# Delta-rule recurrence: level masks put on the products by VectorE, and another order of side work

## What is computed

```python
def rwkv7_branch(z, mu, w0, w_up, a0, a_up, k_k, k_a, r_k, ln_g, ln_b):
    z = token_shift_mix(z, mu)
    r, k, v, g, wd, ad = split_cols(z, RWKV_COLS)
    w = jnp.exp(-DECAY_SCALE * jax.nn.sigmoid((w0 + jnp.tanh(wd) @ w_up).astype(f32)))
    a = jax.nn.sigmoid((a0 + ad @ a_up).astype(f32))
    ...
    kk = kk / jnp.maximum(jnp.linalg.norm(kk, axis=-1, keepdims=True), 1e-12)
    k = k * (1.0 + (a - 1.0) * per_head(k_a))

    def step(state, inp):
        r_t, w_t, k_t, v_t, kk_t, a_t = inp
        sa = jnp.einsum('bhvk,bhk->bhv', state, -kk_t)
        state = (state * w_t[:, :, None, :]
                 + sa[..., None] * (kk_t * a_t)[:, :, None, :]
                 + v_t[..., None] * k_t[:, :, None, :])
        return state, jnp.einsum('bhvk,bhk->bhv', state, r_t)
    ...
    _, y = lax.scan(step, s0, (...))
```

## Time and profile before

| | us |
|---|---|
| median of 3 runs | 4497.86 |
| lowest, highest | 4497.32, 4507.33 |
| profiled execution | 4503.45 |
| its span, first to last instruction | 4502.2 |

### The profile page before, as it was taken

One profiled execution on the slowest core, in us unless ns is written; L12 is line 12 of the kernel. 1 busy time (PEld: TensorE's weight loads), 2 busy tenths in 40 slices (PEclk: granted clock), 3 DMA queues, 4 the chain that ended last, 5 costly groups with the idle time before them and its releaser, 6 DMA issues. The chain is left out here.

```text
span 4502.2 us, 55986 instructions
## 1 busy us (share of the span) xinstructions
PE 3841.9 (85%) x22256; PEld 2253.5 (50%) x22256; DVE 1901.7 (42%) x4026; ACT 1023.9 (23%) x2215; POOL 573.3 (13%) x412
## 2 busy tenths in 40 slices
PE   7699816699999998899986787699899986887698
PEld 1464413344444444565654776344565654776344
DVE  0223375411002111278874553332278974553332
ACT  0321103300001100230123444122230123444122
POOL 0000004200000000002301331110002301331110
PEclk9799958899999999899998888799999998888799
DMA  6212253322442243213321004320213321004320
GB/s 227 89 45 81 76 162 113 132 70 89 149 159 84 82 161 112 69 43 89 94 74 59 25 27 129 113 70 14 65 42 89 94 74 59 25 27 140 102 71 19
DMA packets 226967, 387.52 MB, mean 86 GB/s; under 512 B 33178, under 2 KB 135970, under 8 KB 225706
## 3 DMA queue, kind: packets, MB, share of 16 engines
q1 hardware_dynamic: 217558, 374.11, 25.1%
q10 hardware_dynamic: 9168, 9.98, 0.7%
HBM read 297.11 MB, written 73.31 MB: 82 GB/s over the span
## 5 line engine op out<-in xcount | busy, mean ns | idle before, releaser
L3105 PE MATMUL win_acc<-win_wt,hTl 128*128 128x384 f32 (+3 forms) x3072 | 909.1, 457 | 18.0 <-DMA win_wt<-in_w_in 18.0
L3105 PEld LDWEIGHTS win_acc<-win_wt,hTl 128*128 128x128 f32 x3072 | 561.7, 191 | 360.0 <-DMA win_wt<-in_w_in 18.8
L1480 PE MATMUL mlp_bk<-hTl,mlp_w 128*128 128x512 f32 x1024 | 444.1, 596 | 22.4 <-DMA mlp_scale<-in_norm_g 22.4
L1502 PE MATMUL mlp_bk<-mlp_w,mlp_aT 128*128 128x512 f32 x1024 | 440.3, 592 | 2.3 <-ACT mlp_aT L1385 1.6
L2195 DVE TENSOR_SCALAR_CACHE_REDUCE win_rl<-d_sc,win_mid 128x384 f32<-128x384 f32 (+5 forms) x384 | 363.2, 946 | 40.1 <-DVE win_mid L2203 28.2
L1480 PEld LDWEIGHTS mlp_bk<-hTl,mlp_w 128*128 128x128 f32 x1024 | 195.7, 192 | 268.0 <-issue 245.3
L1502 PEld LDWEIGHTS mlp_bk<-mlp_w,mlp_aT 128*128 128x128 f32 x1024 | 194.2, 190 | 246.3 <-issue 246.3
L1287 DVE TENSOR_SCALAR mlp_r<-mlp_bk,mlp_b 128x512 f32<-128x512 f32 x64 | 48.1, 751 | 494.9 <-PE mlp_bk L1480 484.8
L2950 PE MATMUL tail_wo<-tail_w_out,tail_yT 128*128 128x512 f32 x512 | 234.2, 612 | 20.7 <-DVE tail_yT L2806 20.7
L420 PE MATMUL zin_acc<-zin_wt,hTl 128*128 128x512 f32 (+2 forms) x640 | 228.4, 512 | 0.0
L2961 PE MATMUL tail_wg<-tail_w_gate,tail_xT 128*128 128x512 f32 x512 | 224.4, 592 | 2.5 <-DVE tail_xT L2806 2.5
(11 more groups left out here) (442 smaller groups left out, 5792.7 us busy)
## 6 DMA issues: line engine op xcount, KB each, us to landing
mlp_w<-in_w SPq DMA_DIRECT2D x48, 2048.0 KB, 8.0
win_wt<-in_w_in SPq DMA_DIRECT2D x18, 1536.0 KB, 8.9
ada_w<-in_w_ada SPq DMA_DIRECT2D x12, 2048.0 KB, 7.6
s_z<-win_ot SPq DMA_DIRECT2D x14, 1536.0 KB, 7.2
hTl<-s_z SPq DMA_DIRECT2D x16, 832.0 KB, 4.6
win_zp<-win_ot SPq DMA_DIRECT2D x8, 1344.0 KB
zin_wt<-in_w_in SPq DMA_DIRECT2D x4, 2048.0 KB, 8.2
tail_w_out<-in_w_out SPq DMA_DIRECT2D x4, 2048.0 KB, 13.6
```

The source lines that it names most:

```text
L1480: mm = pe.matmul(bk[:, 4 * half + f % 2, :], wv[:, k, f * P:(f + 1) * P], hT[:, k, half * HT * P:(half + 1) * HT * P], start=k == 0, stop= ...
L1502: mm = pe.matmul(bk[:, bank(n0 + t_) + q, :], aT[:, 4 * c + f, group(2 * pair + t_)], wv[:, f, q * COL:(q + 1) * COL], start=c == 0 and f ...
L3105: mm = pe.matmul(acc[:, u % RING, 0:w], hT[:, k, t * P:(t + 1) * P], wt[:, i % 2, k, 0:w], start=k == 0, stop=k == KC - 1)
```

## The change

GpSimd no longer cuts L to its levels: `lower`, LT and its semaphore go. `make_P` multiplies the whole matrix that `first_pairs` leaves in mT (now I - L, written in place), and `take_P` multiplies the product by the level's mask, whose constant now holds the diagonal too. `first_pairs` computes I - L and then masks it, so it has two instructions as before. `ends` also waits for `r6_ready`, the last piece of `keys`. On VectorE the side work is in another order: exponents, three keys, take_tr, three keys, scaled; `rates(n+1)` goes ahead of the masks. `take_S` and `take_y` move to ScalarE. ScalarE's side work starts at step 3: two exponentials, take_r2, two exponentials, take_S 0, nothing, nothing, take_S 1, take_y; `low` goes ahead of `turn_in`. On TensorE `turn_low(n+1)` goes ahead of the turns and `low(n+1)` ahead of values. At the start, exponents(0) go ahead of keys(0).

```diff
             def _(gp):
-                def lower(n):
-                    for g in range(NG):
-                        hs = slice(2 * g, 2 * g + 2)
-                        gp.wait_ge(masked, START + n * RWH + 2 * g + 2)
...
-                        gp.tensor_tensor(LT[:, q, :, :], mT[:, n % 2, :, 0, :], bc_mid(levels[:, q, :], RWH), ALU.mult).then_inc(LT_ready, 1)
...
                 def ends(m):
...
+                    gp.wait_ge(r6_ready, START + m + 1)
                     gp.wait_ge(f_ready, START + m + 1)
...
                 gp.wait_ge(const_in, START + N_CONST * DMA)
-                ends(0)
                 for n in range(NT):
-                    lower(n)
-                    if n + 1 < NT:
-                        ends(n + 1)
+                    ends(n)
...
                 def first_pairs(n, g):
-                    TT = Tb[:, n % 2, g, 1, :, :]
+                    L = mT[:, n % 2, 2 * g:2 * g + 2, 0, :]
                     dve.wait_ge(masked, START + n * RWH + 2 * g + 2)
-                    tt(TT, mT[:, n % 2, 2 * g:2 * g + 2, 0, :], bc_mid(first[:, :], 2), ALU.mult)
-                    dve.tensor_tensor(TT, TT, bc_mid(id64[:, :], 2), ALU.add).then_inc(TT_first, 1)
+                    s(dve.scalar_tensor_tensor(L, L, -1.0, bc_mid(id64[:, :], 2), ALU.mult, ALU.add))
+                    dve.tensor_tensor(Tb[:, n % 2, g, 1, :, :], L, bc_mid(first[:, :], 2), ALU.mult).then_inc(TT_first, 1)
...
                 def take_P(n, k):
-                    g = k % NG
+                    q, g = divmod(k, NG)
                     dve.wait_ge(p_made, START + n * K + k + 1)
-                    dve.scalar_tensor_tensor(PS[:, 2 * g:2 * g + 2, :], blocks(bk[:, k % 2, 0:2 * HD]), -1.0, bc_mid(id64[:, :], 2),
-                                             ALU.mult, ALU.add).then_inc(p_out, 1)
+                    dve.tensor_tensor(PS[:, 2 * g:2 * g + 2, :], blocks(bk[:, k % 2, 0:2 * HD]), bc_mid(levels[:, q, :], 2),
+                                      ALU.mult).then_inc(p_out, 1)
...
                 def side(n):
                     ahead, behind = n + 1 < NT, n >= 1
-                    yield from keys(n + 1) if ahead else range(6)
+                    early = keys(n + 1) if ahead else iter(range(6))
+                    yield from exponents(n + 1) if ahead else range(4)
+                    yield from islice(early, 3)
                     yield from take_tr(n - 1) if behind else range(1)
-                    yield from exponents(n + 1) if ahead else range(4)
-                    yield from take_S(n - 1, 0) if behind else range(1)
-                    yield
-                    yield from take_S(n - 1, 1) if behind else range(1)
+                    yield from early
                     if ahead:
                         yield from scaled(n + 1)
-                    if behind:
-                        yield from take_y(n - 1)
...
                 rates(0)
+                for _ in exponents(0):
+                    pass
                 dve.wait_ge(const_in, START + N_CONST * DMA)
                 for _ in keys(0):
                     pass
-                for _ in exponents(0):
-                    pass
...
                 for n in range(NT + 1):
+                    if n + 1 < NT:
+                        rates(n + 1)
                     if n < NT:
                         mask(n, 0)
                         mask(n, 1)
                         first_pairs(n, 0)
-                    if n + 1 < NT:
-                        rates(n + 1)
-                    if n < NT:
                         mask(n, 2)
...
+                def take_S(n, c):
+                    pr, po = half(c)
+                    act.wait_ge(zeroed, START + 1)
+                    act.wait_ge(S_made, START + 2 * n + c + 1)
+                    act.activation(St[po, :], bk[po, 6, 0:RW], ACT.Copy).then_inc(S_ready, 1)
+                    yield
+
+                def take_y(n):
+                    act.wait_ge(S_made, START + 2 * n + 2)
+                    if n >= 4:
+                        act.wait_ge(stored[n % 4], START + n // 4 * DMA)
+                    act.activation(yo[:, n % 4, 0:RW], bk[:, 7, 0:RW], ACT.Copy).then_inc(y_read, 1)
+                    yield
...
                 def side(n):
-                    yield from take_r2(n - 1) if n >= 1 else range(1)
-                    yield
-                    yield
-                    yield
-                    if n + 1 < NT:
-                        yield from exps(n + 1)
+                    ahead, behind = n + 1 < NT, n >= 1
+                    curves = exps(n + 1) if ahead else iter(range(4))
+                    yield from islice(curves, 2)
+                    yield from take_r2(n - 1) if behind else range(1)
+                    yield from curves
+                    if behind:
+                        yield from take_S(n - 1, 0)
+                        yield
+                        yield
+                        yield from take_S(n - 1, 1)
+                        yield from take_y(n - 1)
...
                             for k in range(K):
                                 take_T(n, k)
-                                if k >= 4:
+                                if k >= 3:
                                     next(rest, None)
...
                 def make_P(n, k):
-                    q, g = divmod(k, NG)
-                    pe.wait_ge(LT_ready, START + (NG + LV - 1) * n + (g + 1 if q == 0 else NG + q))
+                    g = k % NG
...
-                            mm = pe.matmul(bk[pr, k % 2, col(h)], LT[pr, q, 2 * g + h, :], T_of(n, 2 * g + h, pr), start=True, stop=True)
+                            mm = pe.matmul(bk[pr, k % 2, col(h)], mT[pr, n % 2, 2 * g + h, 0, :], T_of(n, 2 * g + h, pr), start=True, stop=True)
...
                     ahead, behind = n + 1 < NT, n >= 1
+                    if ahead:
+                        turn_low(n + 1)
                     if n < NT:
                         turns(n)
                     if ahead:
-                        turn_low(n + 1)
+                        low(n + 1)
                     if behind:
                         values(n - 1)
```

More of the change, by code:

```diff
@@ L4 @@
 import numpy as np
-from itertools import chain
+from itertools import chain, islice
 import concourse.bass as bass
@@ L1621, in rwkv @@
         Tb = ph.sb("Tb", [P, 2, NG, 2, 2, HD])
-        LT, PS = ph.sb("LT", [P, LV, RWH, HD]), ph.sb("PS", [P, RWH, HD])
+        PS = ph.sb("PS", [P, RWH, HD])
         wv, uw = ph.sb("wv", [P, 3, RWH, P]), ph.sb("uw", [P, RWH, P])
@@ L1630, in rwkv @@
         names = ("wd_turned wdT_ready lowrank pre sig cums cums_out ex_ready fn_ready f_ready x4_ready "
-                 "r6_ready ext_ready turned xT_ready scores masked TT_first T_turned LT_ready p_made p_out t_made t_out "
+                 "r6_ready ext_ready turned xT_ready scores masked TT_first T_turned p_made p_out t_made t_out "
                  "dv_made dv_ready uw_made uw_ready half_made last_made tr_ready r2_ready S_made S_ready y_read zeroed").split()
         (wd_turned, wdT_ready, lowrank, pre, sig, cums, cums_out, ex_ready, fn_ready, f_ready, x4_ready,
-         r6_ready, ext_ready, turned, xT_ready, scores, masked, TT_first, T_turned, LT_ready, p_made, p_out, t_made, t_out,
+         r6_ready, ext_ready, turned, xT_ready, scores, masked, TT_first, T_turned, p_made, p_out, t_made, t_out,
          dv_made, dv_ready, uw_made, uw_ready, half_made, last_made, tr_ready, r2_ready, S_made, S_ready, y_read, zeroed) = (ph.sem(n) for n in names)
@@ L1938, in _ @@
                             turn_in(n, q)
-                    if n + 1 < NT:
-                        low(n + 1)
                     if 1 <= n <= NT:
@@ L1964, in turn_low @@
                     pe.wait_ge(in_[m % 4], START + (m // 4 + 1) * 2 * DMA)
+                    if m >= 1:
+                        pe.wait_ge(cums_out, START + m)
                     if m >= 3:
@@ L2129, in _ @@
                         score(n, 1)
-                    if ahead:
-                        low(n + 1)
-                    if n < NT:
                         score(n, 2)
@@ L3318, in constants_2 @@
     pair = (s // 2 == t // 2)
-    c["rw_first"] = -halves(pair & (s < t)).astype(f)
-    c["rw_levels"] = np.stack([halves((s // (2 * b) == t // (2 * b)) & (s % (2 * b) < b) & (t % (2 * b) >= b)) for b in (2, 4, 8, 16, 32)], 1).astype(f)
+    c["rw_first"] = halves(pair & (s <= t)).astype(f)
+    c["rw_levels"] = np.stack([halves((s // (2 * b) == t // (2 * b)) & (s % (2 * b) >= b) & (t % (2 * b) < b) | (s == t)) for b in (2, 4, 8, 16, 32)], 1).astype(f)
     c["causal_ts"] = np.where(t <= s, 0, -BIG).astype(f)
```

2 lines of the change are left out of this document (removed).

## The result

The change makes the kernel faster: a median of 4391.26 us (4387.34 to 4394.88, four runs) against 4500.44 for the kernel before in the same comparison, a ratio of 0.9755 with a 95% interval of 0.9738 to 0.9772. The gain is 109 us; 4414 was forecast, with 4394 as the low end of the range. The direction and the main mechanism held; the size of the gain was forecast too small.

What follows compares the result with a forecast made beforehand. TensorE's order of work bounds the recurrences. Per layer 5.0 + 20.7 + 16.5 + 1.5 + 0.7 - 0.65 = 43.75 us, twice 87.5, off 4503.45: 4416, given as 4414; range 4394 to 4458 for 8 in 10.

Steps and rivals of the forecast that it cites:

- What bounds the kernel: In the recurrences of both layers, TensorE's order of work is the path, and its gaps are what can be won.
- Masks: Level multiplies leaving GpSimd, some 95 us of its work: 0 gain outside the head, bounds 4 us either way.
- Chain of blocks 1 to 6: The 15 steps of make_P to take_T in six blocks per layer: 3.45 us less each, 20.7 per layer.
- First chain: The first block's chain, which has no chunks: 15.9 us against 20.9, 5.0 less per layer.
- Head: Turns, scores, low-rank and sums products before a chain: 1.2 us less by order, 1.55 by clock; six give 16.5 per layer.
- Last head: The eighth block's head: 1.5 us less per layer, from the clock alone.
- Clock: TensorE's longest idle stretch, 1.2 us before make_T(9), leaves the clock up; if up in the head, 1.55 us less there.
- the rival at 4436: Clock falls as before in the heads, taking back 1.55 us seven times per layer, 21.7; chance 0.25.
- The copies: State and output copies on ScalarE: hidden by the wait for scaled; without that cover up to 0.5 us a block.
- ScalarE as the bound: Its queue in steps 3 to 12 delays take_T and the last exponential: slower, 4547 us; chance 0.06.
- the table load: ScalarE's load before exponentials takes 1.28 us; the skill's 1.38 drain per switch would add 20 us in all, making 4434.
- The shorter wait: Scaled 1 goes earlier than C+14.6 (C: block's first make_P), tail at TensorE's pace: 1.5 us more per block, 4393; chance 0.10.

Runs made afterwards that it cites:

- The filled kernel: The kernel before with 12, 2 and 2 idle identity matmuls put ahead of make_T(12), (13) and (14), nothing left out: 4468.35 us, ratio 0.9929.

## Why the forecast was 23 us too high

- **What bounds the kernel**: right. TensorE's order is the path, and its gaps were what went. What paces the tail of the chain was wrong: the prediction had the steps behind make_T(9) "go by VectorE", and the 6.0 us from there to the next turns came out nearly right (5.8), although TensorE waited for VectorE only 0.5 us of them. Its own carry and steps take nearly as long; that is luck.
- **Masks**: 0 outside the head, with bounds of 4 us either way. Measured 8 us, and 1.3 of a layer's share (1.9 in the new order) in the first block, which has no chunks to hide it under. TensorE's waits for LT, on which I rested the 0, showed nothing of what GpSimd does to VectorE's durations. That shows in VectorE's 59.5 us too: 26.5 are the copies, and 16.7 of the rest two multiplies of `keys` that had run beside the masks. Groups by line (count, busy us, mean ns, idle), first before, then after:

```profile
L1730 DVE SCALAR_TENSOR_TENSOR rwkv_t<-rwkv_la,rwkv_rows 128x384 f32<-128x384 f32 x16 | 18.8, 1177 | 2.0 <-issue 2.0
```

```profile
L1716 DVE SCALAR_TENSOR_TENSOR rwkv_t<-rwkv_la,rwkv_rows 128x384 f32<-128x384 f32 x16 | 8.8, 549 | 0.0
```

- **Chain of blocks 1 to 6**: right. 3.45 each was forecast, 20.7 per layer; measured 22.1 and 21.2. The stretch that I took as 24.97 was 24.83 in most blocks, and the new one is 21.38 for 21.5.
- **First chain**: 5.0 forecast, 4.1 measured (20.64 to 16.53). I had read 20.9.
- **Head: the term that was mis-sized.** 2.75 a block, 16.5 per layer; measured 21.7 and 24.2. It failed twice. First, the base: the earlier trace rows shows the block at 2572.00 with 11.9, and that is the shortest of the twelve heads; their mean is 12.45. That is 0.55 twelve times, 6.6 us. Second, the new head: 9.15 forecast (11.9 less 2.75), 8.63 measured, 0.52 twelve times, 6.2 us. Against the mean head, 1.07 is missing: 0.65 of it the clock, 0.2 the order, and 0.2 between the two, which I put down to the masks. In the block that I read, the clock was back by 2576.0, 4 us into the head. In another, whose turns start at 2645.93, it came back later, as these half microseconds of the kernel before show:

```profile
2645.93:2646.43 0.50, 0.50 (x3) 0.50 (x4) 0.00 (x0) 0.00 (x0) 0.39 (x1) 0.50 0.80 293
...
2650.00:2650.50 0.50, 0.50 (x17) 0.50 (x19) 0.00 (x0) 0.04 (x1) 0.00 (x0) 0.50 0.00 0
2650.50:2651.00 0.50, 0.50 (x15) 0.34 (x8) 0.00 (x0) 0.48 (x2) 0.00 (x0) 0.80 0.00 0
```

  There it is some 4.8 us into the head, and that head took 12.46; over the twelve heads it is 3.6 to 5.4 us. The filled kernel shows the whole price, 2.2, for the 1.55 that I took as half of three operations. The order gave 1.42 for 1.2. The sum had a flaw here too: it ended the sigmoid at T+7.1 and then took the clock's 1.55 off the head, although the sums behind that sigmoid and what follows them take 2.7 us more, so that C couldn't come before T+9.8. The sigmoid came sooner: it ended at T+5.9, and TensorE waited 0.06 us for it. The 0.8 to spare that was forecast isn't there.
- **First head**: 0.7 forecast, 0.7 and 0.9 measured. **Last head**: 1.5 forecast, 2.75 measured: 2.3 of it the clock, by the filled kernel. **Eighth chain and drain**: 0 forecast, 0.65 measured. **Start**: 0.65 lost in the forecast, 0.4 measured.
- **Clock**: "if it stays up" was right, and with it the bet that 1.2 us of idle time leaves it up. The kernel with the copies on VectorE shows that this isn't sure for waits of 1.44 us: there the rival at 4436 came in for four blocks of twelve.
- **The copies**: the prediction called them hidden on ScalarE, and asked only what they cost there. Off VectorE they free the queue around scaled; with them there, the medians are 12.6 us higher, 8.5 of it in the recurrences. The forecast's chain had them on ScalarE already, so its sum holds, but the gain was not named.
- **ScalarE as the bound** (4547): didn't come. It is 11.05 of 21.38 us busy in the chain, and three exponentials ahead of take_r2 made the kernel faster still. On **the table load** the row settles it: load at 2625.84, exponential at 2627.14, so 1.28 and no drain behind it. The 1.38 us more per switch that the Trainium skill gives (ScalarE: Activation LUTs, What ACT_TABLE_LOAD costs) are not seen here either.
- **The shorter wait** (4393) gave nearly the measured time, but not by its mechanism: the last exponential was where the forecast had it. Its price was off as well: nine parts of 0.71 are 6.4 us, 0.5 less than the 6.9 and not 1.5. The kernel with the ends behind scaled measured that, 0.44.

In sum: per layer the heads gave 5.2 and 7.7 us more than forecast, the last head and drain 1.9, the full chains 0.9 on average, first head, first chain and start together 0.6 less. That is 8.7 per layer, twice 17.4, and the phases show 104.9 for 87.5. Of the 22.7 us between 4414 and the measured median, 4.3 lie outside the phases, in code that is the same, and 1 in the level from which the forecast counted.

## What to carry to other kernels

A term that is taken twelve times wants the mean of the twelve, not one block: list the length of each repeat first. Where the clock falls at the end of a block, price it with the stretch until it is back at 1.00 in several blocks, or measure it by filling the gap with matmuls that nobody reads. And when a side engine's instructions double in length, look for what runs beside them before looking at queues.

## What was not expected of the hardware

- Idle matmuls in a gap of 3.3 us gave the kernel before 32 us: the level of 1.2 GHz that followed the gap cost 2.2 us of each head of 12.45.
- A gap of 1.43 or 1.44 us at the same place of ten chains was followed by the low level in four of them; gaps of 1.08 in the changed kernel's twelve full chains never were, nor was one of 1.63 in another version.
- A float32 multiply of 128x384 with both inputs in SBUF took 0.55 us alone on VectorE, 1.03 to 1.35 beside GpSimd's; GpSimd's took 1.00 alone and 1.27 to 1.32 beside it. Keeping them apart shortened VectorE's chain work by 1.6 us, the chain by 0.44.
